# Interleaving long and short query tiles in the attention of the second block

## What is computed

```python
# latent attention, layer 0 (8 heads)
o_x = blockwise_attend(q_x, concat([k_c, k_x]), concat([v_c, v_x]), scale)   # 768 keys
o_c = dense_attend(q_c, k_c, v_c, scale)                                     # 256 keys
# windowed attention, layer 1 (16 heads): softmax with a sink column
s_band = where(|qpos - kpos| <= 128, q_x . k_band, -1e30)                    # up to 384 keys
s_ctx  = q_x . k_c                                                           # 256 keys
o_x = sink_attend([s_ctx, s_band], [v_c, v_band], sink)
o_c = sink_attend([q_c . k_c], [v_c], sink)                                  # 256 keys
```

## Time and profile before

| | us |
|---|---|
| median of 3 runs | 3759.04 (3753.53 to 3760.4) |
| profiled execution, its own time | 3761.22 |
| span of its trace, first to last instruction | 3759.5 |
| mla attention of layer 0 | 1551.4 to 1746.2 |
| swa attention of layer 1 | 2092.4 to 2269.3 |

### The profile page before, as it was taken

One profiled execution on the slowest core, in us unless ns is written; L12 is line 12 of the kernel. 1 busy time (PEld: TensorE's weight loads), 2 busy tenths in 40 slices (PEclk: granted clock), 3 DMA queues, 4 the chain that ended last, 5 costly groups with the idle time before them and its releaser, 6 DMA issues. The chain is left out here.

```text
span 3759.5 us, 35670 instructions
## 1 busy us (share of the span) xinstructions
PE 3133.9 (83%) x13906; PEld 1859.3 (49%) x13906; DVE 1133.2 (30%) x2356; ACT 748.6 (20%) x1675; POOL 253.5 (7%) x286
## 2 busy tenths in 40 slices
PE   7999975787776788988898888899867683988898
PEld 3458643444443655665455554556533242364564
DVE  3441621000000201233310682433038686310242
ACT  2112710000000202332200571100011110112331
POOL 0000001000000000000000000011014141000000
PEclk9999986888888899999999999999978786999999
DMA  6664327999998111100012100122230104012100
GB/s 224 232 232 138 121 75 240 366 362 365 360 366 304 56 51 37 65 1 23 1 34 68 68 1 1 45 92 85 71 128 6 34 31 144 38 40 56 67 1 23
DMA packets 247042, 437.03 MB, mean 116 GB/s; under 512 B 27641, under 2 KB 108057, under 8 KB 246908
## 3 DMA queue, kind: packets, MB, share of 16 engines
q1 hardware_dynamic: 233420, 400.49, 30.5%
q0 software_dynamic: 8368, 26.31, 2.2%
q10 hardware_dynamic: 5120, 8.39, 0.6%
HBM read 401.85 MB, written 32.52 MB: 116 GB/s over the span
## 5 line engine op out<-in xcount | busy, mean ns | idle before, releaser
L1889 PE MATMUL moe_ph<-moe_w,moe_x_T 128*64 128x256 f32 x2048 | 276.3, 430 | 139.0 <-DMA moe_w<-w 120.8
L300 PE MATMUL hyena_in_main<-hT,second_weights 128*128 128x256 f32 (+1 forms) x1024 | 330.5, 486 | 1.4 <-PEq L773 1.4
L1889 PEld LDWEIGHTS moe_ph<-moe_w,moe_x_T 128*64 128x64 f32 x2048 | 162.8, 156 | 255.8 <-issue 180.9
L300 PEld LDWEIGHTS hyena_in_main<-hT,second_weights 128*128 128x128 f32 x1024 | 194.5, 190 | 137.2 <-issue 124.0
L300 PE MATMUL swa_in_main<-hT,second_weights 128*128 128x512 f32 (+1 forms) x576 | 189.4, 489 | 6.6 <-DMA second_weights<-b_w_in 5.2
L1185 PE MATMUL qkv_main<-hT,first_weights 128*128 128x512 f32 (+1 forms) x384 | 167.8, 580 | 0.9 <-PEq L773 0.9
L300 PEld LDWEIGHTS swa_in_main<-hT,second_weights 128*128 128x128 f32 x576 | 109.9, 191 | 86.5 <-issue 73.8
L2002 DVE TENSOR_TENSOR moe_act_rows<-moe_ph,moe_act 128x256 f32<-128x256 f32 x32 | 13.6, 425 | 435.1 <-PE moe_ph L1889 435.1
L509 PE MATMUL mla_att_scores<-mla_kn,mla_qn 128*128 128x256 f32 (+1 forms) x288 | 111.6, 534 | 26.8 <-ACT second_weights L668 18.8
L591 DVE TENSOR_REDUCE mla_att_maxes<-mla_att_scores 128x1 f32<-128x768 f32 (+1 forms) x80 | 64.3, 846 | 196.8 <-PE mla_att_scores L509 196.2
L1911 PE MATMUL moe_py<-moe_w,moe_act_T 128*64 128x512 f32 x512 | 116.9, 598 | 2.1 <-ACT moe_act_T L1983 2.1
(11 more groups left out here) (431 smaller groups left out, 4903.7 us busy)
## 6 DMA issues: line engine op xcount, KB each, us to landing
moe_w<-w SPq DMA_DIRECT2D x96, 2048.0 KB, 16.7
first_w_out<-w_mod SPq DMA_DIRECT2D x12, 2048.0 KB
mixT<-w_mod SPq DMA_DIRECT2D x12, 2048.0 KB, 8.0
first_weights<-w_in SPq DMA_DIRECT2D x16, 1024.0 KB
second_weights<-c_w_in SPq DMA_DIRECT2D x16, 1024.0 KB
second_weights<-b_w_in SPq DMA_DIRECT2D x10, 1024.0 KB
scr_expert_rows<-moe_y ACTq DMA_DIRECT2D x64, 128.0 KB, 6.3
second_weights<-a_w_in SPq DMA_DIRECT2D x7, 1024.0 KB
```

Source lines behind the costliest of these rows:

```text
L300: mm = pe.matmul(main[u][0:unit.rows, 0:unit.cols], lhsT, rhs, start=(c == 0), stop=(c == r.kc - 1))
L1889: mm = pe.matmul(bank[half * T:(half + 1) * T, 0:HF], x_T[s][:, c, :], w[s][:, c, half * HF:(half + 1) * HF], start=(c == 0), stop=(c == K ...
```

## The change

A function gives the order of the tiles inside a pair. With context it is t0, s4, t1, t2, s5, t3; without context it is t0 to t3 as before, so layer 3 is unchanged. Both item loops use it. No instruction is added or removed.

```diff
+def spread_tiles(with_ctx):
+
+    if not with_ctx:
+        return list(range(XT))
+    order, gap = [], XT // CT
+    for t in range(CT):
+        order += [t * gap, XT + t] + list(range(t * gap + 1, (t + 1) * gap))
+    return order
...
         items = []
         for p in range(A_HEADS // 2):
-            for t in range(nq // P):
+            for t in spread_tiles(with_ctx):
...
-            for t in range(XT + CT):
+            for t in spread_tiles(True):
```

## The result

The changed kernel takes 3779.31 us (median of 5 runs, 3778.22 to 3785.04) against 3759.11 us of the kernel before, timed beside it (5 runs, 3753.53 to 3761.62): ratio 1.0056, 95% interval 1.0045 to 1.0068. It is slower by 20.2 us, where 16 was forecast. The profiled execution took 3785.04 us, the longest of the five, with a span of 3783.3.

What follows compares the result with a forecast made beforehand. VectorE was taken as swa's fullest engine (17.7 of 21.37 us a pair), TensorE as mla's pace. The profiled 3761.2 + 16.9 (swa) - 1 (mla) gave 3777; from the median, 3759 + 16 = 3775 us, range 3762 to 3786.

Steps and rivals of the forecast that it cites:

- the release: swa: moment TensorE may write behind a short, 1.16 us after the start of ScalarE's exp of that short.
- the hold: swa: small VectorE operation with two SBUF inputs stands until GpSimd's product ends; 1.7 us a pair where it was 0.65.
- the clock: TensorE's clock: a wait of 1.56 us keeps full speed, 2.55 does not; no half-speed loss summed for swa.
- the walk of swa: swa: new queues followed with row durations, three legs closing a pair; 23.4 us against 21.37, in all +16.9.
- Leg 1: swa: from R to VectorE's start on t2; 5.2 us, or 3.5 if the hold does not grow.
- R: swa: the release of region 0 by s4, where the first leg starts and the third ends.
- The first rival: swa: the hold does not grow, pair 21.7 us, in all +4, 3763 us; chance 0.13.
- Leg 2: swa: from t2's start b to the next pair's t0; 11.5 us, with VectorE idle 1.3.
- Leg 3: swa: from t0's start a to the next R; 6.7 us, with s5's transposes starting at a + 1.66.
- mla: mla: waits +0.87, half-speed stretch -1.69, so -0.8 a pair; last tile +3.3, first pair -2; sum -1 (-4 to +6).
- The third rival: swa and mla: TensorE's clock drops in both stages, mla gives +6 instead of -1, 3782 to 3786 us; chance 0.09.
- The second rival: swa: spread shorts free their regions before anyone asks, -20, 3739 us, decided at exp of s4 and s5; chance 0.07.

Runs made afterwards that it cites:

- new_nogate: The changed kernel with swa's GpSimd gate products left out; 3765.51 us, one run.
- old_nogate: The kernel before with swa's GpSimd gate products left out; 3755.90 us, one run.
- mla_only: The changed kernel with swa put back to its old order, so only mla is reordered; 3759.81 us, ratio 0.9998 to the kernel before.
- new_short_dve: The changed kernel with swa's short items given the mask's zero part, so VectorE copies their logits to SBUF; 3754.75 us, ratio 0.9985 to the kernel before.
- swa_only: The changed kernel with mla put back to its old order, so only swa is reordered; 3786.54 us, ratio 1.0061 to the kernel before.
- old_short_dve: The kernel before with swa's short items given the mask's zero part, so VectorE copies their logits to SBUF; 3750.94 us, ratio 0.9975.

## Why the prediction was right, and where it was off

The forecast said slower, 3775 us (3762 to 3786), and 3779.31 came. The place, swa, and both mechanisms, the release and the hold, were right; their sizes were partly off. Without the clock's share the sums below are 13.7 - 0.3 = +13.4, so the sign did not hang on the clock. It came 4.2 us low because a term of 7.7 for the clock was missing, and it is luck that it was not lower: the walk of swa was 3.2 too high.

- **Leg 1** was 5.2 us by the walk and is 5.08 (2146.93 to 2152.01). GpSimd starts 2.34 behind R, where 2.26 was worked out, and covers L604, as forecast. L602 starts 0.04 ahead of GpSimd there, the case for which the prediction reckoned 0.1 more and left it out of the sum; the product's row is 1.81 long as elsewhere, so no row shows that term. The first rival (the hold does not grow) is refuted: new_nogate and old_nogate price it at 1.19 and 0.64. But the walk had 1.7 for the first (5.2 against 3.5). In new_nogate leg 1 is 3.79 (2143.02 to 2146.81) and not 3.5, and leg 2 11.63. So of the loss in a period the hold is 0.54, where the walk had 1.05.
- **Leg 2** was 11.5 and is 11.52 (2129.01 to 2140.53), with 1.37 us idle on VectorE where 1.3 was worked out.
- **Leg 3** was 6.7 and is 6.40 (2140.53 to 2146.93). From there comes most of the 0.4 by which the period at full clock is under 23.4: s5's transposes start at a + 1.42 (2141.95), where the walk had a + 1.66. The release came 1.17 us after the exp's start (2145.76, on ScalarE), as before.
- **The clock** is the step that failed. "A wait of 1.56 keeps it, one of 2.55 does not" was read from mla and carried to swa. In its full periods the waits stayed under 1.56 (1.32, 0.98 and 0.84 are the longest), and the clock fell all the same, in three of the six full periods. That costs 1.43, 1.57 and 1.58 us over the 23.00. The third rival had this for swa with 0.09, for which it left up to 4 us without a working; its mla part did not come. The Trainium skill (TensorE: Matmul & The Clock Gate, A second HAM failure mode) tells of such short pauses; the prediction had set it aside because no row showed it, and in swa the trace agrees with it.
- **swa's sum.** With these taken off, and 1.57 us for each of the first and last stretches (an estimate from the periods), the first pair is +1.3 (forecast +1.8), the six periods 6 x 1.63 = +9.8 (forecast +12.1), the last +2.6 (forecast +3.0): +13.7, where 16.9 was forecast. The clock adds 7.7. Together they are the measured 21.4. So the errors of swa's walk, all in one direction, hid 3.2 us of the term that the sum did not have.
- **mla.** The pair was to gain 0.8 and gained 47.35 - 46.65 = 0.70 (the 47.35 is 1609.98 to 1657.33 on TensorE before). Its waits are 0.77 and 1.56, where 0.93 and 1.56 were forecast. The last pair loses 3.6 (forecast 3.3 - 0.8 = 2.5), the first gains 2.5 (forecast 2). The stage gains 0.3, where 1 was forecast. Even that gain depends on the execution: the same old order also took 191.4 us (last section), and mla_only can't be told from the kernel before (0.9988 to 1.0007).
- **The second rival** (faster, because spread shorts free their regions in time) was decided where it said. ScalarE reaches the exps of s4 and s5 behind a long exp and copies; only with the release and the hold both taken out is the spread order 0.36 us a pair ahead. With the release alone taken out it stays behind: new_short_dve's stage is 170.6 us against 167.7, since its hold is larger (1.18 against 0.66 a pair) and the last period, ending on a long tile, is 1.7 longer. Its median is 3754.75 against 3750.94, a difference near what such runs can tell.

Open: why three periods lost the clock and three did not. Ahead of 2159.00, where it fell, TensorE waited 0.98, 0.62 and 0.84 us; ahead of 2208.00, where it did not, 0.98, 0.63 and 0.84:

```profile
2204.37 1.12 PE L521 MATMUL swa_att_turned<-const_identity,swa_att_probs 128*128 128x128 f32 x8 [0.98 <-DVE swa_att_probs L623]
...
2208.00 0.48 PE L509 MATMUL swa_att_scores<-swa_qk 64*128 64x256 f32 x1 [0.84 <-ACT swa_att_probs L668]
```

So the waits just ahead don't tell the two apart. Without the hold one such period was left. With the release by VectorE none was, in the new order's two kernels of six full periods each; what else decides is not shown. Between a stage's difference in one profile and the difference of the medians, 2 to 5 us are not followed up (swa_only: stage +21.3, median +26.1; old_short_dve: stage -7.1, median -9.5).

## What to carry to other kernels

A reordering moves no work, so walk the ring of waits that closes a pair, with starts from the rows: three legs of it came within 0.3 us. Legs can hide errors that cancel, so price each part by a kernel that lacks it: the hold cost 1.19 where the walk had 1.7. Then ask what each item is followed by: two of the three losses came because a buffer that is freed by a late engine is now wanted twice a pair, and because the last item of a group is now one whose completion triggers a foreign engine amid small operations. Often the better change is to the buffer and not to the order: freeing the region from VectorE, which reads it anyway, gave 0.9975 in the old order, and neither of the other two orders gave more beyond noise (0.9985 and 0.9974). And where a reordering adds pauses to a TensorE that sits at full clock, put a half-clock term into the sum and not only into a rival.

## What the runs showed of the hardware

- TensorE in swa dropped from 2.4 to 1.2 GHz in three full periods whose longest wait is 1.32 us, and stayed there for some 3 us (0.50 from 2184 to 2187). In mla of the old order the same wait of 2.55 us is followed by eight products in 4.54 us or in 2.85. This is a row of TensorE in old_short_dve, whose mla is the code of before:

```profile
1613.41 2.85 PE L509 MATMUL mla_att_scores<-mla_kn,mla_qn 128*128 128x512 f32 x8 [2.55 <-ACT second_weights L668]
```

 That stage took 191.4 us in two profiled executions and 194.8 in six with the same code. In the new order it took 194.5 in all five.
- A VectorE operation with one SBUF tensor input is held too: L605, 128x2, took 1.79 us beside GpSimd's product instead of 0.16. The prediction spoke of two inputs alone. The Trainium skill (SBUF - State Buffer, Who interferes with whom) names tensor_scalar among the operations that can enter a mode that contends with GpSimd; the row agrees.
- The held operation (128x2 each time, 0.16 us alone) took what was left of GpSimd's instruction: 0.81 to 0.82, 1.33, 1.68 and 1.79 us, by when GpSimd started against it.
